# Gate and up products of an expert block in turn, one pair of weights each, in a diffusion backbone on one core

## The chip, the cores and the metric

The kernel runs on 1 core of one Trainium2 chip. The metric is the device time of one execution in microseconds (us); a median over executions is given, and the profile is of one execution. The computation is all in float32.

## The reference

A two-layer backbone over 256 latent tokens and 256 context tokens of width 1024. Layer 0 mixes by latent attention and pooling and has a dense SwiGLU of width 2816. Layer 1 mixes by a 2-D Fourier transform and has a mixture of eight experts of width 3584, of which each token uses two. A final RMSNorm follows. The case is about the experts:

```python
def swiglu(h, w1, w3, w2):
    return (jax.nn.silu(h @ w1) * (h @ w3)) @ w2

def moe_swiglu(h, router_w, w1, w3, w2):
    logits = (h @ router_w).astype(jnp.float32)
    top_v, top_i = lax.top_k(logits, TOP_K)
    top_p = jax.nn.softmax(top_v, axis=-1)
    gates = jnp.sum(jax.nn.one_hot(top_i, N_EXPERTS, dtype=jnp.float32) * top_p[..., None],
                    axis=-2).astype(h.dtype)
    y = jnp.zeros_like(h)
    for e in range(N_EXPERTS):
        y = y + gates[..., e:e + 1] * swiglu(h, w1[e], w3[e], w2[e])
    return y
```

`w1` gives the gate product, `w3` the up product, `w2` the down product. The weights of one expert are 44 MB, of all eight 352 MB.

## The kernel before

The first 400 us or so compute layer 0, the Fourier mixing of layer 1, the router, and gather the tokens of the first four experts. Then the expert stage begins, and it runs to the end but for some 15 us of final norm and output.

**Places.** The experts are computed in eight places, one after the other, in two groups of four (`expert`, called from line 2412 for the first group and line 2419 for the second). An expert's tokens are gathered into 96 slots, three groups of 32 (`QUAD`). Places 1, 3 and 7 are light: they take 64 slots, two groups of 32. The others are called heavy here. A second round of places, for experts with more tokens, isn't run on these inputs.

**Blocks and pairs.** An expert's width of 3584 is cut into 7 blocks of 512. Of each block, gate, up and down weights are 2 MB each: one pair, of two halves of 1 MB. So an expert has 21 pairs, q = 0 to 20. `PAIR_AT` (line 118) says which are whose. The work of a place is in phases: up(0), the last down of the place before (`down` 3), up(1) with the combine of the place before inside it, down(0), up(2), down(1), up(3), down(2). Phases 0 to 2 have two blocks and phase 3 one. In an up phase the gate pair of a block comes first (q) and the up pair next (q + 1).

**The ring.** Pairs land in a ring of 8 slots (`SLOTS`) in on-chip memory. SP (SyncE) issues all loads in the order of use, each for the slot of the pair eight before it. The pairs of place 0 that have to wait for a slot are loaded by halves (`load_half`, line 637); from place 1 on (and for the last pair of place 0) a load is a whole pair (`load`, line 632). The loads of the first eight pairs are issued before the stage begins. SP waits on the semaphore `e_used`, which TensorE raises: 42 halves (`PIECES`) a place. `used_with` gives the count after which half s of a pair is free.

**Gate and up.** `up` (line 2335) takes both pairs of a block at once: `landed_two` is a view of two slots. The tokens are the stationary operand, 128 rows by 32 columns, and the weights are the moving one, 256 columns: 128 of the gate pair and 128 of the up pair. For each half s of the pairs, four contraction chunks k, the groups g of 32 tokens and four column groups c of the array (each taking other weight columns), there is one matmul (line 2352): 192 a block in a heavy place, 128 in a light one. Gate and up results of up to two blocks stand side by side in one PSUM bank a group, `bank[g]`. Ahead of half s TensorE waits for both pairs (`pair_wait` twice), and after it `e_used` rises by 2. So both pairs of a block come free together, and SP needs no wait of its own for the second of them (`QUAD_SECOND`).

**Down.** `down` multiplies the hidden values with one pair at a time, 512 columns a matmul (line 2367), into banks 3 and 4, and raises `e_used` by 1 a half.

**Between them.** When the last block of an up phase is done (`up_done`), ScalarE takes silu of the gate side (line 1048), VectorE multiplies with the up side (line 1708) and transposes (line 1712). The first matmul of a bank in the next up phase waits for the multiplication (`e_hidden`). A place's output is taken from the banks, multiplied with the gate values and spread back to the tokens (line 2331). Line 2321 gathers tokens. Line 1777 is a product of layer 0 with 128 moving columns. Line 1039 loads a place's gate table, from ScalarE's queue.

Of the kernel before, what the change touches and what calls it, by code (L numbers as in the profile page):

```python
# [15 lines left out]
P = 128  # L16
D = 1024
KD = D // P
# [101 lines left out]
QUAD_FIRST = tuple(at for (phase, *_), at in PAIR_AT.items() if phase == "up")  # L120
QUAD_SECOND = tuple(at + 1 for at in QUAD_FIRST)

# [93 lines left out]
def build(nc, vec_d, con_d, rope_d, x_d, ctx_d, ada_d, mixa_d, mixb_d, attn_d, mixout_d, ffn_d,  # L216
          dft_d, fnet_d, router_d, moe_d, out_d):
    ctx = ExitStack()
    with ctx:
# [29 lines left out]
        def view(t, at, *dims):  # L249

            n = int(np.prod(dims))
            v = t[:, at:at + n]
            if len(dims) == 2:
                return v.rearrange("p (a b) -> p a b", a=dims[0])
            if len(dims) == 3:
                return v.rearrange("p (a b c) -> p a b c", a=dims[0], b=dims[1])
            return v
# [194 lines left out]
        def queue_at(i, q):  # L452

            return PAIRS * i + q - 1 if i or q >= AHEAD else q
# [26 lines left out]
        def used_with(q, s, last):  # L481

            if q in QUAD_FIRST:
                return 2 * last + (2 if s == 0 else 4)
            return 2 * last + (s + 1 if q not in QUAD_SECOND else 2 * s)
# [41 lines left out]

        def landed_two(slot):

            pairs = view(ring, 0, SLOTS, 2 * PIECE)  # L530
            one, other = SLOT_AT[slot], SLOT_AT[(slot + 1) % SLOTS]
            return pairs[:, one:other + 1, :] if other > one else pairs[:, one::other - one, :]
# [57 lines left out]
        def _(sp):  # L590
# [93 lines left out]
            def expert_loads(e, before, i, group, j):  # L684

                for q in range(PAIRS):
                    if q == 0 and j == 0 and not isinstance(group, int):
                        sp.wait_ge(e_used, PIECES * i - 2)
                    elif (q + PAIRS - SLOTS) % PAIRS not in QUAD_SECOND:
                        sp.wait_ge(e_used, PIECES * i + used_with((q + PAIRS - SLOTS) % PAIRS, 1, q - SLOTS - 1))  # L690
                    load(slot_of_pair(group, j, q), before if q == AHEAD else e, q)
# [3 lines left out]
            for (phase, *_), q in PAIR_AT.items():  # L695
                for s, n in ([(s, queue_at(0, q) + d) for s in range(2) for d in range(2)] if phase == "up" else
                             [(s, queue_at(0, q) + d) for d in range(1 if q == AHEAD else 2) for s in range(2)]):
                    if SLOTS <= n < BY_HALVES and q != AHEAD:
                        left = n - SLOTS
                        sp.wait_ge(e_used, used_with(left if left < AHEAD else left + 1, s, left))  # L700
                        load_half(n, s)
# [11 lines left out]
            freed = sp.value_load(loops[0:1, 2:3], min_val=PIECES * EXPERTS - 2 * SLOTS + 2, max_val=PIECES * EXPERTS * MAX_ROUNDS)  # L713
# [370 lines left out]
        def _(dve):  # L1084
# [435 lines left out]
            def cols(at, n):  # L1520
                return small[:, at:at + n]
# [89 lines left out]
            def gates():  # L1611
# [27 lines left out]
                link(nc.vector.tensor_scalar(cols(213, 1), cols(210, 1), float(PIECES * EXPERTS), float(PIECES * EXPERTS - 2 * SLOTS + 2),  # L1639
# [118 lines left out]
        def _(pe):  # L1758
# [576 lines left out]
            def up(i, j, phase, block, first, light, group):  # L2335

                blocks = 1 if phase == 3 else 2
                q = PAIR_AT["up", phase, block]
                weights = landed_two(slot_of_pair(group, j, q)).rearrange("p z (s k h a c r) -> p z s k h a c r", s=2, k=4, h=2, a=2, c=2)
                for s in range(2):  # L2340
                    if j == 0 and phase == 0 and block == 0:
                        pe.wait_ge(x_first, KD // 2 * group + 2 * s + 2)
                        pe.wait_ge(x_second, KD // 2 * group + 2 * s + 2)
                    for side in range(2):
                        pair_wait(pe, group, j, q + side, s)
                    for k in range(4):
                        for g in range(slots_of(light)):
                            if block == 0 and s == 0 and k == 0 and not (first and phase == 0):
                                pe.wait_ge(e_hidden, PHASES * TRIPLES * i + TRIPLES * (phase - 1) + g + 1)
                            for c in range(4):  # L2350
                                out = bank[g][c * QUAD:(c + 1) * QUAD, 0:2 * blocks * P].rearrange("p (z b n) -> p z b n", z=2, b=blocks)
                                last = mm(out[:, :, block, :].rearrange("p z (a r) -> p z a r", a=2),  # L2352
                                          x_group[:, 4 * s + k, j * CAP + g * QUAD:j * CAP + (g + 1) * QUAD],
                                          weights[:, :, s, k, c // 2, :, c % 2, :],
                                          start=(block == 0 and s == 0 and k == 0), stop=(s == 1 and k == 3 and block == blocks - 1), skip_group_check=True)
                    last.then_inc(e_used, 2)
# [140 lines left out]
```

## Time and profile before

| What | us |
|---|---|
| Median of 3 runs | 1247.53 |
| Lowest and highest | 1246.42, 1248.97 |
| The profiled execution | 1248.82 |
| Span of its profile | 1247.0 |

The page of a profile gives each engine's busy time, then the span in 40 equal slices (31.2 us each) with the rate of the transfers, the DMA queues, the chain of work that ended last, and groups of instructions by line. "PE" is TensorE's matmuls, "PEld" its weight loads, "SPq" SP's queue of DMA issues. In a group, "x9408" is a count, then come busy time and the mean length of one; matmuls overlap, so busy time divided by the count is the pace of them, and the mean length is more. "Idle before" is idle time of the engine ahead of the group, with what ended it. In the chain, "issue" is time in which the engine waited for nothing that the profile shows. A wait for two semaphores is put down to one of them.

Of the DMA queues, q1 holds what SP issues (weights), q10 what ScalarE issues (gate tables), q8 the instructions of the program. "DMA to landing" is the time from SP's issue of a load until all of it is in.

### The profile page before, as it was taken

The page shows a single profiled execution, that of the slowest core. Times are in us where ns is not written, and L with a number is a line of the kernel's source. Part 1 is how long each engine was busy: PE and PEld are TensorE (multiplying, and loading weights), DVE is VectorE, ACT ScalarE, POOL GpSimd, SP SyncE. Part 2 cuts the span into 40 slices and gives each one's busy share as a digit, 9 for nine tenths or more (in the row PEclk, how much of TensorE's full clock was granted, in tenths as well). Part 3 has the DMA queues.
Part 4 walks back from the last instruction along what each step waited for, and adds up shares of the span by engine and source line. Part 5 has one row for each costly group of instructions (what it writes and reads, how often), then busy time and mean ns, then how long its engine had stood idle before and what let it go on. Part 6 is the DMA issues. An engine that isn't in the chain of part 4 may idle for free.

```text
span 1247.0 us, 33411 instructions
## 1 busy us (share of the span) xinstructions
PE 1189.7 (95%) x15405; PEld 766.4 (61%) x15405; DVE 429.7 (34%) x853; ACT 222.9 (18%) x375; POOL 16.6 (1%) x34
## 2 busy tenths in 40 slices
PE   8999999999999999998999997799999999999977
PEld 6767999999997654453555554455555545555533
DVE  3588699999866101010020020112002011200203
ACT  4375543334433000000000000000000000000002
POOL 0400000000000000000000000000000000000000
PEclk8999999999999999998999999899999999999989
DMA  9963799988845899999999999999999999999992
GB/s 385 350 240 110 274 390 357 356 342 333 329 172 203 353 377 382 422 420 427 426 425 426 426 424 428 427 423 427 426 425 422 399 418 405 414 403 425 425 426 119
DMA packets 39548, 460.08 MB, mean 369 GB/s; under 512 B 4592, under 2 KB 4976, under 8 KB 7024
## 3 DMA queue, kind: packets, MB, share of 16 engines
q1 hardware_dynamic: 38064, 455.77, 88.9%
q8 instruction: 122, 2.00, 0.6%
q10 hardware_dynamic: 1344, 2.16, 0.5%
q14 instruction: 18, 0.15, 0.0%
HBM read 456.81 MB, written 1.11 MB: 367 GB/s over the span
## 4 chain that ended last, share of the span: by engine, by line
PE 70%; DVE 14%; DMA 11%; issue 3%; ACT 1%; DVEq 0%; SPq 0%; ACTq 0%
PE bank L2352 37%; PE bank L2367 18%; DMA ring<-in_moe 9%; DVE work L1161 6%; DVE split L1145 4%; PE bank L1885 4%; PE bank L1957 1%; PE bank L1777 1%; PE bank L2331 1%; PE bank L2321 1%; DMA ring<-in_ada 1%; DMA ring<-in_fnet 1%; DVE ring L1435 1%; DVE split L1446 1%; PE bank L2093 1%
## 5 line engine op out<-in xcount | busy, mean ns | idle before, releaser
L2352 PE MATMUL bank<-ring,work 128*32 128x256 f32 x9408 | 525.9, 384 | 36.6 <-issue 22.1
L2352 PEld LDWEIGHTS bank<-ring,work 128*32 128x32 f32 x9408 | 313.5, 111 | 254.0 <-issue 65.3
L2367 PE MATMUL bank<-ring,moe 128*32 128x512 f32 x2352 | 258.2, 592 | 0.0
L1708 DVE TENSOR_TENSOR moe<-moe,bank 128x256 f32<-128x256 f32 (+1 forms) x84 | 28.2, 384 | 621.8 <-ACT moe L1048 621.8
L2367 PEld LDWEIGHTS bank<-ring,moe 128*32 128x32 f32 x2352 | 77.6, 110 | 161.6 <-issue 154.5
L1048 ACT ACTIVATE moe<-bank 128x256 f32<-128x256 f32 (+1 forms) x84 | 24.4, 357 | 746.2 <-PE bank L2352 746.2
L2178 PE MATMUL bank<-split 128*128 128x256 f32 x1024 | 125.4, 283 | 0.8 <-DVE split L1145 0.7
L2178 PEld LDWEIGHTS bank<-split 128*128 128x128 f32 x1024 | 123.8, 192 | 1.6 <-DVE split L1145 1.2
L1145 DVE TENSOR_TENSOR split<-ring,split 128x2048 fp32r<-128x2048 f32 x33 | 75.5, 2289 | 7.4 <-ACT split L941 3.3
L1161 DVE SCALAR_TENSOR_TENSOR work<-ring,condp,work 128x512 f32<-128x512 f32 x98 | 73.6, 752 | 4.1
L941 ACT ACTIVATE split<-ring 128x2048 fp32r<-128x2048 f32 x31 | 59.3, 1914 | 74.8 <-PE bank L2178 72.6
L2168 PE MATMUL bank<-split 128*128 128x256 f32 x480 | 59.4, 283 | 0.0
L2168 PEld LDWEIGHTS bank<-split 128*128 128x128 f32 x480 | 58.3, 192 | 0.4 <-issue 0.4
L1885 PE MATMUL bank<-split 128*128 128x256 f32 x384 | 47.5, 284 | 0.0
L1885 PEld LDWEIGHTS bank<-split 128*128 128x128 f32 x384 | 46.4, 192 | 1.4 <-issue 1.4
L1694 DVE SCALAR_TENSOR_TENSOR xT<-bank,ada,xT 128x256 f32<-128x256 f32 x64 | 25.9, 476 | 53.5 <-PE bank L2331 53.5
L1100 DVE TENSOR_TENSOR split<-ring,split 128x1024 fp32r<-128x1024 f32 (+1 forms) x24 | 27.8, 1175 | 7.5 <-ACT split L786 7.2
L786 ACT ACTIVATE split<-ring 128x1024 fp32r<-128x1024 f32 (+1 forms) x24 | 24.0, 1017 | 32.4 <-PE bank L1885 18.2
L1712 DVE STREAM_TRANSPOSE moe<-moe 128x256 f32<-128x256 f32 (+1 forms) x84 | 28.2, 382 | 0.0
L1957 PE MATMUL bank<-split 128*128 128x256 f32 x168 | 25.8, 305 | 1.1 <-ACT split L815 0.9
L1957 PEld LDWEIGHTS bank<-split 128*128 128x128 f32 x168 | 21.6, 189 | 4.0 <-issue 3.5
L1686 DVE SCALAR_TENSOR_TENSOR split<-bank,small,split 128x512 fp32r<-128x512 f32 x16 | 11.3, 747 | 30.5 <-ACT split L1023 30.5
(279 smaller groups left out, 619.3 us busy)
## 6 DMA issues: line engine op xcount, KB each, us to landing
ring<-in_moe SPq DMA_DIRECT2D x148, 2048.0 KB, 23.6
ring<-in_moe SPq DMA_DIRECT2D x40, 1024.0 KB, 8.9
ring<-in_ffn SPq DMA_DIRECT2D x16, 2048.0 KB, 8.1
ring<-in_ada SPq DMA_DIRECT2D x28, 1024.0 KB, 7.1
ring<-in_ada SPq DMA_DIRECT2D x10, 2048.0 KB, 10.1
ring<-in_mixout SPq DMA_DIRECT2D x2, 2048.0 KB, 8.2
ring<-in_fnet SPq DMA_DIRECT2D x2, 2048.0 KB, 10.0
ring<-in_mixa SPq DMA_DIRECT2D x2, 1024.0 KB, 15.9
```

The source lines that it names most:

```text
L941: nc.scalar.activation(high_d[:, q % SPLITS_DENSE, :], piece_view(q), ACT.Copy).then_inc(high_ready, 1)
L1100: nc.vector.tensor_tensor(mixer_part(m, 1), mixer_source(m), plain(mixer_part(m, 0)), ALU.subtract).then_inc(mixer_low, 1)
L1145: nc.vector.tensor_tensor(low_d[:, q % SPLITS_DENSE, :], piece_view(q), plain(high_d[:, q % SPLITS_DENSE, :]), ALU.subtract).then_inc(low_ ...
L1161: ins = nc.vector.scalar_tensor_tensor(out=total, in0=half_view(h)[:, k, :], scalar=weight, in1=total, op0=ALU.mult, op1=ALU.add)
L1708: nc.vector.tensor_tensor(gate_e[:, g, 0:n], gate_e[:, g, 0:n], bank[g][:, n:2 * n], ALU.mult).then_inc(e_hidden, counts_for(light, g))
L1712: nc.vector.transpose(hiddenT[phase % 2][:, g, 0:n].rearrange("p (a s r) -> p a s r", s=2, r=QUAD), gate_e[:, g, 0:n].rearrange("p (a r s) ...
L1885: last = mm(bank[banks[c // 2]][:, (c % 2) * T:(c % 2) * T + T], parts[left][:, k, j * P:(j + 1) * P], source[right][:, k0 + k, :], start= ...
L1957: last = mm(out, parts[left][:, k, lo:hi], h_in[right][:, k0 + k, 0:n], start=((left, right) == PRODUCTS[0] and k0 + k == 0 and opens), st ...
L2168: last = mm(bank[FFN_BANKS[k // 2]][:, (k % 2) * T:(k % 2) * T + T], w[:, j, k * P:(k + 1) * P], hidden_parts[g % 2][:, right, j, :], star ...
L2178: last = mm(bank[kind == "w3"][:, j * T:(j + 1) * T], w[:, k, j * P:(j + 1) * P], h_parts[:, right, k, :], start=(n == 0 and j == 0 and k ...
L2352: last = mm(out[:, :, block, :].rearrange("p z (a r) -> p z a r", a=2), x_group[:, 4 * s + k, j * CAP + g * QUAD:j * CAP + (g + 1) * QUAD] ...
L2367: last = mm(bank[3 + n][c * QUAD:(c + 1) * QUAD, :], hiddenT[phase % 2][:, g, blk * QUAD:(blk + 1) * QUAD], weights[:, s, j, n * 512:(n + ...
```

## The change

The gate product of a block is computed in full from its pair, and then the up product from the other: the loop over `side` is outside the loops over halves and chunks. A matmul has 128 columns in place of 256, and there are twice as many. Each half waits for its own pair alone and raises `e_used` by 1. The columns at which results stand in PSUM stay the same. `QUAD_FIRST`, `QUAD_SECOND` and `landed_two` go, `used_with` becomes a plain count, SP waits before every load, and the halves of place 0 are loaded in plain order. The constant for the very last load follows the new count.

```diff
-        def used_with(q, s, last):
-
-            if q in QUAD_FIRST:
-                return 2 * last + (2 if s == 0 else 4)
-            return 2 * last + (s + 1 if q not in QUAD_SECOND else 2 * s)
+        def used_with(last, s):
+
+            return 2 * last + s + 1
...
                 for q in range(PAIRS):
                     if q == 0 and j == 0 and not isinstance(group, int):
                         sp.wait_ge(e_used, PIECES * i - 2)
-                    elif (q + PAIRS - SLOTS) % PAIRS not in QUAD_SECOND:
-                        sp.wait_ge(e_used, PIECES * i + used_with((q + PAIRS - SLOTS) % PAIRS, 1, q - SLOTS - 1))
+                    else:
+                        sp.wait_ge(e_used, PIECES * i + used_with(q - SLOTS - 1, 1))
                     load(slot_of_pair(group, j, q), before if q == AHEAD else e, q)
...
-            for (phase, *_), q in PAIR_AT.items():
-                for s, n in ([(s, queue_at(0, q) + d) for s in range(2) for d in range(2)] if phase == "up" else
-                             [(s, queue_at(0, q) + d) for d in range(1 if q == AHEAD else 2) for s in range(2)]):
-                    if SLOTS <= n < BY_HALVES and q != AHEAD:
-                        left = n - SLOTS
-                        sp.wait_ge(e_used, used_with(left if left < AHEAD else left + 1, s, left))
-                        load_half(n, s)
+            for n in range(SLOTS, BY_HALVES):
+                for s in range(2):
+                    sp.wait_ge(e_used, used_with(n - SLOTS, s))
+                    load_half(n, s)
...
             def up(i, j, phase, block, first, light, group):
 
                 blocks = 1 if phase == 3 else 2
-                q = PAIR_AT["up", phase, block]
-                weights = landed_two(slot_of_pair(group, j, q)).rearrange("p z (s k h a c r) -> p z s k h a c r", s=2, k=4, h=2, a=2, c=2)
-                for s in range(2):
-                    if j == 0 and phase == 0 and block == 0:
-                        pe.wait_ge(x_first, KD // 2 * group + 2 * s + 2)
-                        pe.wait_ge(x_second, KD // 2 * group + 2 * s + 2)
-                    for side in range(2):
-                        pair_wait(pe, group, j, q + side, s)
-                    for k in range(4):
-                        for g in range(slots_of(light)):
-                            if block == 0 and s == 0 and k == 0 and not (first and phase == 0):
-                                pe.wait_ge(e_hidden, PHASES * TRIPLES * i + TRIPLES * (phase - 1) + g + 1)
-                            for c in range(4):
-                                out = bank[g][c * QUAD:(c + 1) * QUAD, 0:2 * blocks * P].rearrange("p (z b n) -> p z b n", z=2, b=blocks)
-                                last = mm(out[:, :, block, :].rearrange("p z (a r) -> p z a r", a=2),
-                                          x_group[:, 4 * s + k, j * CAP + g * QUAD:j * CAP + (g + 1) * QUAD],
-                                          weights[:, :, s, k, c // 2, :, c % 2, :],
-                                          start=(block == 0 and s == 0 and k == 0), stop=(s == 1 and k == 3 and block == blocks - 1), skip_group_check=True)
-                    last.then_inc(e_used, 2)
+                for side in range(2):
+                    q = PAIR_AT["up", phase, block] + side
+                    weights = landed(slot_of_pair(group, j, q)).rearrange("p (s k h a c r) -> p s k h a c r", s=2, k=4, h=2, a=2, c=2)
+                    for s in range(2):
+                        if j == 0 and phase == 0 and block == 0 and side == 0:
+                            pe.wait_ge(x_first, KD // 2 * group + 2 * s + 2)
+                            pe.wait_ge(x_second, KD // 2 * group + 2 * s + 2)
+                        pair_wait(pe, group, j, q, s)
+                        for k in range(4):
+                            for g in range(slots_of(light)):
+                                if block == 0 and side == 0 and s == 0 and k == 0 and not (first and phase == 0):
+                                    pe.wait_ge(e_hidden, PHASES * TRIPLES * i + TRIPLES * (phase - 1) + g + 1)
+                                for c in range(4):
+                                    at = (side * blocks + block) * P
+                                    last = mm(bank[g][c * QUAD:(c + 1) * QUAD, at:at + P].rearrange("p (a r) -> p a r", a=2),
+                                              x_group[:, 4 * s + k, j * CAP + g * QUAD:j * CAP + (g + 1) * QUAD],
+                                              weights[:, s, k, c // 2, :, c % 2, :],
+                                              start=(block == 0 and side == 0 and s == 0 and k == 0),
+                                              stop=(s == 1 and k == 3 and block == blocks - 1), skip_group_check=True)
+                        last.then_inc(e_used, 1)
```

## Rows read from the trace of the kernel before

**Rows 1.** The page, its head and TensorE's busy time
```profile
span 1247.0 us, 33411 instructions
...
PE 1189.7 (95%) x15405; PEld 766.4 (61%) x15405; DVE 429.7 (34%) x853; ACT 222.9 (18%) x375; POOL 16.6 (1%) x34
```

**Rows 2.** The page, GB/s moved in each of the 40 slices
```profile
GB/s 385 350 240 110 274 390 357 356 342 333 329 172 203 353 377 382 422 420 427 426 425 426 426 424 428 427 423 427 426 425 422 399 418 405 414 403 425 425 426 119
```

**Rows 3.** Engines by windows, place 0, with clock, DMA share and GB/s
```profile
core 0: us, PE busy (x) PEld busy (x) DVE busy (x) ACT busy (x) POOL busy (x), PEclk, DMA share, GB/s
400.00:410.00 10.00, 10.00 (x183) 5.97 (x185) 5.40 (x29) 3.13 (x4) 0.00 (x0) 1.00 0.31 104
410.00:420.00 10.00, 10.00 (x192) 6.00 (x187) 0.00 (x0) 0.00 (x0) 0.00 (x0) 1.00 0.81 306
...
440.00:450.00 10.00, 10.00 (x133) 4.10 (x128) 2.09 (x6) 0.94 (x3) 0.00 (x0) 1.00 0.81 278
```

**Rows 4.** The chain that ended last: start, length, what
```profile
484.99 10.36 PE bank L2352 x192
...
571.46 4.98 issue
...
1181.67 29.42 DMA ring<-in_moe
...
1211.32 9.90 PE bank L2352 x128
1221.21 10.35 PE bank L2367 x96
```

**Rows 5.** TensorE's groups by line from 808 to 1109 us
```profile
L2352 PE MATMUL bank<-ring,work 128*32 128x256 f32 x3840 | 209.9, 379 | 0.0
```

**Rows 6.** Groups of the whole span; the third is one burst on the timeline
```profile
L2352 PE MATMUL bank<-ring,work 128*32 128x256 f32 x9408 | 525.9, 384 | 36.6 <-issue 22.1 <-DMA ring<-in_moe 13.5 <-DVE moe L1708 1.1
...
L1777 PE MATMUL bank<-ring,condp 128*32 128x128 f32 x512 | 17.0, 287 | 0.2 <-DMA ring<-in_ada 0.2
...
22.49 1.96 PE L1777 MATMUL bank<-ring,condp 128*32 128x128 f32 x64
```

**Rows 7.** Line 632's loads: issued from 500.5, at 500.7, at 1197.5, and all
```profile
L632 SPq DMA_DIRECT2D ring<-in_moe x142: 332/333/1462, 500.7 to 1197.5; - x142
DMA to landing us min/median/max: 10.6/24.0/36.2
...
DMA to landing us min/median/max: 14.3/14.3/14.3
...
DMA to landing us min/median/max: 28.3/28.3/28.3
...
DMA to landing us min/median/max: 7.6/23.6/36.2
```

**Rows 8.** DMA queues from 500 to 1226 us, then q8 of the whole span
```profile
q1 hardware_dynamic: 20670, 300.92, 98.2%
q10 hardware_dynamic: 1008, 1.84, 0.7%
q8 instruction: 81, 1.33, 0.7%
...
q8 instruction: 122, 2.00, 0.6%
```

**Rows 9.** DMA queues from 600 to 900 us: packets, MB, share of 16 engines
```profile
q1 hardware_dynamic: 8672, 126.32, 99.2%
q8 instruction: 34, 0.56, 0.8%
q10 hardware_dynamic: 432, 0.79, 0.7%
```

**Rows 10.** By windows, the end of the last load (columns as in rows 3)
```profile
1221.00:1223.00 2.00, 2.00 (x24) 0.61 (x20) 1.32 (x6) 0.45 (x2) 0.00 (x0) 1.00 0.54 229
1223.00:1225.00 2.00, 2.00 (x24) 0.58 (x20) 0.53 (x2) 0.00 (x0) 0.00 (x0) 1.00 0.16 66
```

More of the change, by code:

```diff
@@ L119 @@
            ("up", 2, 0): 11, ("up", 2, 1): 13, ("down", 1): 15, ("up", 3, 0): 17, ("down", 2): 19}
-QUAD_FIRST = tuple(at for (phase, *_), at in PAIR_AT.items() if phase == "up")
-QUAD_SECOND = tuple(at + 1 for at in QUAD_FIRST)
 Y_ROWS = ((1, 1, 2, 0), (0, 1, 2, 2))
@@ L526, in landed @@
             return view(ring, SLOT_AT[slot] * 2 * PIECE, 2 * PIECE)
[L528 to L532, printed above, removed]
         def by_rows(t, f):
@@ L712, in _ @@
                             expert_loads(seated(GROUP * side + j), before, GROUP * group + j, group, j)
-            freed = sp.value_load(loops[0:1, 2:3], min_val=PIECES * EXPERTS - 2 * SLOTS + 2, max_val=PIECES * EXPERTS * MAX_ROUNDS)
+            freed = sp.value_load(loops[0:1, 2:3], min_val=PIECES * EXPERTS - 2 * SLOTS, max_val=PIECES * EXPERTS * MAX_ROUNDS)
             last = seated(EXPERTS - 1)
@@ L1638, in gates @@
                 link(nc.vector.tensor_scalar(cols(212, 1), cols(210, 1), 1.0, None, ALU.add))
-                link(nc.vector.tensor_scalar(cols(213, 1), cols(210, 1), float(PIECES * EXPERTS), float(PIECES * EXPERTS - 2 * SLOTS + 2),
+                link(nc.vector.tensor_scalar(cols(213, 1), cols(210, 1), float(PIECES * EXPERTS), float(PIECES * EXPERTS - 2 * SLOTS),
                                              ALU.mult, ALU.add))
```

## The prediction, made before the changed kernel was run

> **What bounds the kernel now.** I read the page first: TensorE is busy 95% of 1247.0 us, which looks like its limit [rows 1], but from about 500 us to the end the transfers run at one flat level, 422 to 428 GB/s in most slices [rows 2]. That stretch is the expert stage, which must bring in the expert weights in pairs of 2 MB through a ring of 8 slots. So two things can bound it: the transfers, or TensorE, which gives the slots back. The table by windows shows which at its start: 104, 306 and 278 GB/s in three stretches of 10 us in which TensorE is fully busy [rows 3]. There the DMA engines wait for slots. The chain of waits then shows the rest. In place 0 (96 tokens' columns) one block of gate and up takes 10.36 us for 192 matmuls, 54.0 ns each. In the light places TensorE waits for transfers: a load is in at 571.46, and from there comes "issue" of 4.98 us, about the time of one more pair: the block waits for both of its pairs, and the second lands 4.9 us after the first [rows 4]. From 808 to 1109 us (places 4, 5 and most of 6) TensorE never waits [rows 5]; at the end it waits again, for a load issued at 1181.67, until 1211.09 [rows 4].
>
> How full are the transfers? From 500 to 1226 us the DMA engines spend 98.2% on weights, 0.7% on gate tables, 0.7% on instructions [rows 8]. And the landings give the pace: the load issued at 500.7 took 14.3 us (landed 515.0), the last, issued at 1197.5, took 28.3 (1225.8), and there are 142 of them: 710.8 / 141 = 5.04 us per pair [rows 7]. So the end is set by the pace of landings, also through the heavy places, and TensorE has 1225.8 to 1231.6 left to do after it [rows 4].
>
> **The change, part by part.** Gate and up of a block are multiplied one after the other, each from its own pair, 128 columns a matmul; a slot is handed back when its own pair has been read, and a pair is waited for alone.
>
> *Matmul time.* 9408 gate/up matmuls of 256 columns [rows 6] become 18,816 of 128, with as many weight loads. The same form (128x32 stationary, 128 columns) is in the trace: 64 in 1.96 us [rows 6]. Taking off the 0.29 us of the last one's own length and dividing by the 15 steps between groups of four gives 0.111 us a step, 28 ns each, against 27.0 ns for half of a 54.0 ns matmul. Low bound: no difference. High bound: 1.96 / 64 = 30.6 ns. I take 28: a block in a heavy place takes 0.4 us more, 2.7 us for the seven of a place. It stays under the transfers' pace where these bind. Its only part on the path is place 0, where it delays the last hand-backs by 0 to 2.7 us; I take 1, nearer the low end, since a burst of 16 steps includes its own start. The Trainium skill (TensorE: Matmul & The Clock Gate, Back-to-back issue gap) says that in a stream of loads and matmuls the spacing is set by both, 81 ns at 128 columns where the isolated gap would be 56. That speaks against this change; by that ratio the 27.0 ns would be 39, an estimate. The trace does not agree for this form, in which four column groups are used side by side: 28 ns against 27.0.
>
> *Slots handed back earlier (gain).* Now both pairs of a block come free together; after, the first comes free half a block (5.2 us) sooner, and in the first 12 loads of place 0, cut in halves of 1 MB, each half after 2.6 us. TensorE frees a pair each 5.2 us in place 0, slower than the transfers need, so after the change the queue stays almost empty there and a load lands as fast as any: 7.6 us is the least in the trace. Before, the load issued at 500.7, at the end of place 0, took 14.3 [rows 7]. That is a lead of 6.7 us when the light place 1 starts and the transfers begin to bind. Off it go the 1 us above and 1.5 us for an instruction fetch that may be in front of a load on its engine: 4.2 us. High bound 6.7; low bound 2.7, if only the half block (5.2) is won and both come off it. Later in the stage hand-backs are not what binds: before 1109 the loads queue for 20 us and more, median 24.0 [rows 7]. SP now waits before each load, where the second of a block's pairs needed no wait; behind it on SP stand only later weight loads, each needing a later release, so nothing is held up. ACT's and VectorE's waits are for the end of a block's last pair, as before: nothing.
>
> *Instructions (loss).* 9408 more matmuls and 9408 more weight loads make 18,816 more instructions beside 33,411 [rows 1]. These 33,411 came in 122 packets of 16 KB on the same DMA engines [rows 8], 274 each. After place 0 there are 8064 of the 9408 matmuls (each heavy place has 1344), so 16,128 more instructions, 59 more packets, in a stretch whose engines are 99.6% taken by the three queues [rows 8]. Price of a packet: the 81 packets there took 0.7% of 16 engines in 726 us, 1.0 us each. Evenly spread that is 1.0 / 16 = 0.063 us of the pace per packet, 3.7 us: the low bound. But a pair has landed only when all 16 engines have done their part. In the 300 us from 600, 126.32 MB took 99.2 of 100.7 parts of the time, so a pair alone costs 300 x 0.985 / 60.2 = 4.91 us [rows 9]; the landings came every 5.04. The excess is 0.13 x 141 = 18.6 us; tables are 0.7% of 726 = 5.1; 13.5 us are left for 81 packets, 0.17 us each. A few engines carry the fetches and are late: at the end of the last load the rate falls in steps, 229 GB/s, then 66, before it stops [rows 10]. I take 0.17: 59 x 0.17 = 10.0 us later. High bound 0.2 (11.8 us), if the tables spread evenly.
>
> *The wait split in two.* In the starved places TensorE starts a block 4.9 us sooner, on its first pair, and then waits in the middle of it: the stall moves to the second pair and nothing comes earlier, since the next pair is not there. Place 4's start does come sooner, but the landings bound the end. Only the last block counts. Now it starts at 1211.32, at a clock that has fallen (9.90 us for 128 matmuls), and 96 matmuls of 10.35 us follow [rows 4]; TensorE is done 5.8 us after the last landing. After, half of the block is done before its second pair lands, and what must follow the last landing is one pair of the down product, a third of 10.35 = 3.5 us. Gain 2.3 us; low bound a loss of 1.1 (that pair at half clock, 6.9 us), if the new waits in between let the clock fall.
>
> **Sum.** 10.0 - 4.2 - 2.3 = +3.5 us on the profiled execution's 1248.82 us (1247.0 of span, 1.8 around it). The median of the three runs, 1247.53, lies 1.3 below that, so I forecast 1251.0 for the median. By the spacing that the Trainium skill gives, TensorE would set the end, as in the third rival below. With all bounds: 3.7 - 6.7 - 2.3 = -5.3 to 11.8 - 2.7 + 1.1 = +10.2.
>
> **The rivals.** (1) *Faster: the earlier slots win.* If the added packets spread over all 16 engines, or fall on those that are early, they cost 3.7 us, and the lead (6.7) and the tail (2.3) outweigh them: -5.3, 1242.2 us. It decides below 0.11 us a packet. For it: only the even 1.0 us of a packet; against it: the excess in the landings and the stepped end. (2) *No change:* near 0.11 us a packet the terms cancel, 6.5 - 4.2 - 2.3 = 0, 1247.5 us. (3) *Weight loads set TensorE's pace:* with half the columns to a load, the load of the next group can set the step; at 30.6 ns the 4032 matmuls of the three heavy places 4 to 6 take 7.2 ns more each, +29 us on a TensorE that has no idle there [rows 5], less about 3 of its earlier start: some 1273. It decides from about 28 ns on, where 2.0 ns x 4032 less 3 is 5 us, as much as the landings lose. By the spacing of the Trainium skill (same page and section) it would be 12 ns a matmul of 128 columns, 97 us, an estimate. Against: the row gives 28 once its ends are taken off, but it is a burst of 64, not a stream of 768. (4) *TensorE runs out of instructions:* 274 now last 137 matmuls of 54 ns (7.4 us), after 3.7 us. If a fetch turns round in more than 3.7 us, each of 59 or more packets costs up to another 3.7, so up to 218 us. Nothing in the trace shows the turn-round, only that 7.4 us is enough.
>
> **How the numbers follow.** Forecast (slower by about 3.5) 0.48; rival 1 0.22; rival 2 0.20; rival 3 0.06; rival 4 0.04. 0.2% is 2.5 us, about what a measurement can tell from no change. Faster 0.22, same 0.20, slower 0.58. The range goes from rival 1's time, 1 us inside it, to the forecast's upper bound, 1247.5 + 10.2 = 1258, and 4 us into the start of rivals 3 and 4: 1243 to 1262.
>
> **What the profile will show.** Right: gate/up matmuls x18816 of 128x128 with a block near 10.6 us; no slice under 380 GB/s between 410 and 500 us; loads issued near 500 us landing in 8 to 10 us; some 195 instruction packets; landings every 5.1 us after 515; TensorE ending 3.5 us after the last landing. Wrong: the same number of packets or a landing pace still at 5.04 (rival 1), TensorE's block over 11.5 us (rival 3), TensorE idle on "issue" inside blocks with its slots landed (rival 4).

## The result and the profile after

The changed kernel takes 1446.17 us (median of 4 runs), against 1247.23 us for the kernel before beside it: 1.159 of the time, interval [1.157, 1.161]. It is 199 us slower, where 3.5 were forecast. Its profiled execution has a span of 1440.1 us.

The page after, its head, the 40 slices (36.0 us each) and the instruction queue:

```profile
span 1440.1 us, 52188 instructions
PE 1252.9 (87%) x24813; PEld 1040.2 (72%) x24813; DVE 430.5 (30%) x853; ACT 222.9 (15%) x375; POOL 17.3 (1%) x34
...
GB/s 361 338 176 176 391 349 363 337 314 198 300 260 340 286 335 383 400 426 366 267 295 362 405 426 400 317 254 291 350 326 270 303 367 255 285 326 371 403 401 39
...
q8 instruction: 195, 3.19, 0.8%
...
PE 72%; issue 13%; DVE 12%; ACT 1%; DMA 1%; DVEq 0%; SPq 0%; ACTq 0%
...
ring<-in_moe SPq DMA_DIRECT2D x148, 2048.0 KB, 9.6
```

Against [rows 1, 2, 8]: 18,777 more instructions in 73 more packets, near what was counted beforehand (18,816 more instructions; 59 packets after place 0, where 64 came: 145 from 525 us on, against 81). But the flat 425 GB/s of the expert stage is gone (254 to 426), and a load lands in a median of 9.6 us where it queued for 24.0 [rows 7]. So the transfers have stopped being the bound. The chain that ended last has 1% of DMA left and 13% of "issue", time in which TensorE waits for nothing that the profile shows.

TensorE's groups from 400 to 1426 us, where the expert stage lies (x count, busy us, mean ns, then idle before and its releaser):

```profile
L2339 PE MATMUL bank<-ring,work 128*32 128x128 f32 x18816 | 579.0, 281 | 155.8 <-issue 154.2 <-DVE moe L1695 1.0
L2355 PE MATMUL bank<-ring,moe 128*32 128x512 f32 x2352 | 279.2, 612 | 10.1 <-issue 10.1
```

Gate and up take 579.0 + 155.8 = 734.8 us where they took 525.9 + 36.6 = 562.5 [rows 6]: 172 us more, of which 119 us are idle time, nearly all of it on "issue", and 53 us busy time. The down product, whose instructions are unchanged, took 258.2 us busy with no idle before; now it takes 289.3, 31 us more. Together that is 203 us, about the whole of the loss (193 of span). In these groups no wait ends with the landing of a load any more. A part of the busy time is the clock: the one granted was 0.96 in the mean from 500 to 1100 us, and behind a row of stops it falls. The 128 matmuls from 680.24 us took 5.20 us, with a mean of 0.72 granted from 680 to 686 us, so a part of it at the lower level of 1.2 GHz; most stretches of 128 take 3.70.

Where in the code does TensorE stop? Its timeline in place 2 of the changed kernel:

```profile
644.25 3.70 PE L2339 MATMUL bank<-ring,work 128*32 128x128 f32 x128 [2.79 <-issue]
650.46 3.70 PE L2339 MATMUL bank<-ring,work 128*32 128x128 f32 x128 [2.51 <-issue]
656.67 3.70 PE L2339 MATMUL bank<-ring,work 128*32 128x128 f32 x128 [2.51 <-issue]
662.06 3.37 PE L2339 MATMUL bank<-ring,work 128*32 128x128 f32 x115 [1.69 <-issue]
665.16 0.59 PE L2355 MATMUL bank<-ring,moe 128*32 128x512 f32 x1
665.23 0.31 PE L2339 MATMUL bank<-ring,work 128*32 128x128 f32 x3
665.33 1.71 PE L2355 MATMUL bank<-ring,moe 128*32 128x512 f32 x9
667.72 2.35 PE L2355 MATMUL bank<-ring,moe 128*32 128x512 f32 x19 [0.68 <-issue]
```

A word on counts first: the loops of `up` make 96 float32 matmuls a block in a heavy place, and the trace records 192, two for each; all counts of matmuls here are the trace's, and so are the instructions. TensorE runs 128 matmuls and stops, time after time, at places that have nothing to do with a half (96 matmuls of 128 columns), a pair (192) or a block (384). With their 128 weight loads these are 256 instructions, and a packet of 16 KB has room for 256 if one is 64 bytes; the page's counts give 52188 / 195 = 268 for all engines. The starts are 6.21 us apart, and 3.70 us of that are work. The count runs on across the lines: 115 + 1 + 3 + 9 = 128 matmuls of both products, then the next stop, inside the down product. The queue of instructions (q8) keeps the same time: its packets stand at 641.8, 648.0, 654.2 and 659.6 us, each within 0.2 us, which is 2.3 to 2.5 us ahead of the four starts, and the second and third come just when the stretch before has ended (647.95 and 654.16). So my reading: the program arrives in packets, one at a time, and TensorE uses one up in 3.5 us. Here a period is the work on one packet and then the fetch of the next. The reading was tested as theory 1, against theory 2, that the single waits and hand-backs of the pairs cost the time.

### The profile page after: what moved, and what is told of

The parts are those of the page before. It is cut to its first block, busy times and chain, and to the rows that moved or that the text cites. A ratio compares the mean times of both kernels' runs of the same rounds, so it can differ in the third digit from the quotient of the medians.

```text
span 1440.1 us, 52188 instructions
## 1 busy us (share of the span) xinstructions
PE 1252.9 (87%) x24813; PEld 1040.2 (72%) x24813; DVE 430.5 (30%) x853; ACT 222.9 (15%) x375; POOL 17.3 (1%) x34
## 4 chain that ended last, share of the span: by engine, by line
PE 72%; issue 13%; DVE 12%; ACT 1%; DMA 1%; DVEq 0%; SPq 0%; ACTq 0%
PE bank L2339 39%; PE bank L2355 18%; DVE work L1148 5%; DVE split L1132 4%; PE bank L1872 3%; PE bank L1944 2%; PE bank L2318 1%; PE bank L1764 1%; PE bank L2308 1%; DMA ring<-in_fnet 1%; DVE ring L1422 0%; DVE split L1433 0%; PE bank L2080 0%; DVE work L1146 0%; PE bank L2066 0%
## 5 line engine op out<-in xcount | busy, mean ns | idle before, releaser
L2339 PE MATMUL bank<-ring,work 128*32 128x128 f32 x18816 | 579.0, 281 | 155.8 <-issue 154.2
L2339 PEld LDWEIGHTS bank<-ring,work 128*32 128x32 f32 x18816 | 543.6, 113 | 197.5 <-issue 191.0
L2355 PE MATMUL bank<-ring,moe 128*32 128x512 f32 x2352 | 279.2, 612 | 10.1 <-issue 10.1
L2355 PEld LDWEIGHTS bank<-ring,moe 128*32 128x32 f32 x2352 | 125.4, 113 | 137.9 <-issue 100.4
L2165 PE MATMUL bank<-split 128*128 128x256 f32 x1024 | 125.4, 283 | 0.9 <-DVE split L1132 0.9
L2155 PE MATMUL bank<-split 128*128 128x256 f32 x480 | 59.4, 283 | 0.0
L1872 PE MATMUL bank<-split 128*128 128x256 f32 x384 | 47.5, 284 | 0.0
L1087 DVE TENSOR_TENSOR split<-ring,split 128x1024 fp32r<-128x1024 f32 (+1 forms) x24 | 27.8, 1176 | 7.5 <-ACT split L773 7.2
L773 ACT ACTIVATE split<-ring 128x1024 fp32r<-128x1024 f32 (+1 forms) x24 | 24.0, 1017 | 28.9 <-PE bank L1872 18.2
L1944 PE MATMUL bank<-split 128*128 128x256 f32 x168 | 25.8, 305 | 1.1 <-ACT split L802 0.9
L2318 PE MATMUL bank<-split 128*128 128x256 f32 x128 | 19.3, 306 | 3.4 <-issue 1.8
```

Of the source, the lines that this page charges most:

```text
L1872: last = mm(bank[banks[c // 2]][:, (c % 2) * T:(c % 2) * T + T], parts[left][:, k, j * P:(j + 1) * P], source[right][:, k0 + k, :], start= ...
L1944: last = mm(out, parts[left][:, k, lo:hi], h_in[right][:, k0 + k, 0:n], start=((left, right) == PRODUCTS[0] and k0 + k == 0 and opens), st ...
L2155: last = mm(bank[FFN_BANKS[k // 2]][:, (k % 2) * T:(k % 2) * T + T], w[:, j, k * P:(k + 1) * P], hidden_parts[g % 2][:, right, j, :], star ...
L2165: last = mm(bank[kind == "w3"][:, j * T:(j + 1) * T], w[:, k, j * P:(j + 1) * P], h_parts[:, right, k, :], start=(n == 0 and j == 0 and k ...
L2318: last = mm(bank[PART_BANKS[pair]][:, (k % 2) * T:(k % 2) * T + T], y_parts[n][:, k * P:(k + 1) * P], spread[:, k // 4, :], start=(n == 0) ...
L2339: last = mm(bank[g][c * QUAD:(c + 1) * QUAD, at:at + P].rearrange("p (a r) -> p a r", a=2), x_group[:, 4 * s + k, j * CAP + g * QUAD:j * C ...
```

## The experiments

### The kernel before with twice the instructions

```diff
-                            for c in range(4):
+                            for z, c in ([(z, c) for z in range(2) for c in range(4)] if True else [(None, c) for c in range(4)]):
...
-                                          weights[:, :, s, k, c // 2, :, c % 2, :],
...
+                                    moving = weights[:, z, s, k, c // 2, :, c % 2, :]
```

> The kernel before, with its pairs, waits and hand-backs as they were; only each gate/up matmul of 256 columns is two of 128, one after the other for the four column groups: 18816 matmuls and 18816 weight loads. Theory 1, TensorE runs out of instructions (a packet of 256 instructions lasts 3.5 us of products and a new one comes each 5.4 to 6.2 us): as slow as the changed kernel, 1425 to 1460 us, with idle on 'issue' after each 128 matmuls. Theory 2, the single pair waits and hand-backs cost the time: as the kernel before, 1245 to 1255 us.

Measured: 1449.93 us (one run, as all that are given here without an interval), the slow-down in full, beside 1246.06 for the kernel before. Its groups:

```profile
L2359 PE MATMUL bank<-ring,work 128*32 128x128 f32 x18816 | 585.0, 284 | 174.5 <-issue 173.0 <-DVE moe L1708 1.0
L2372 PE MATMUL bank<-ring,moe 128*32 128x512 f32 x2352 | 266.2, 596 | 5.7 <-issue 5.7
```

Waits and hand-backs are those of before, and the idle time on "issue" is there. The order of gate and up, and the single pairs, are not needed for it.

### The changed kernel with as few instructions as before

```diff
-                        for k in range(4):
+                        for k in (0, 2):
...
-                                              weights[:, s, k, c // 2, :, c % 2, :],
+                                              weights[:, s, k:k + 2, c // 2, :, c % 2, :],
```

> The changed kernel with its single pair waits and hand-backs, but each gate/up matmul reads 256 columns of two contraction chunks of one pair, with the tokens of the first of the two, so that there are 9408 again, of the time of before. It leaves out the products of the odd chunks with their own tokens and puts them in other columns. Theory 1: no slow-down; the earlier hand-backs and the split wait show alone, 1239 to 1247 us. Theory 2: 1400 us or more.

Measured: 1241.28 us, 0.9962 of the kernel before, interval [0.9948, 0.9976]. Theory 2 is dead: with all the single waits and hand-backs of the change, and 9408 matmuls, the kernel is 4.8 us faster than before. Its windows in place 0 and its loads issued between 495 and 506 us:

```profile
400.00:410.00 10.00, 10.00 (x192) 6.04 (x188) 4.05 (x22) 1.49 (x2) 0.00 (x0) 1.00 0.78 288
410.00:420.00 10.00, 9.32 (x176) 5.33 (x164) 0.19 (x1) 0.61 (x3) 0.00 (x0) 1.00 0.99 390
...
440.00:450.00 10.00, 10.00 (x112) 3.51 (x108) 2.09 (x6) 0.94 (x3) 0.00 (x0) 1.00 0.99 358
```

```profile
L622 SPq DMA_DIRECT2D ring<-in_moe x2: 332/332/333, 498.7 to 503.9; - x2
DMA to landing us min/median/max: 9.8/9.9/10.0
```

The three stretches that moved 104, 306 and 278 GB/s [rows 3] now move 288, 390 and 358, and a load at the end of place 0 lands in 9.9 us in place of 14.3 [rows 7]: a lead of 4.4 us, where 4.2 was forecast. The landing itself, of the 142nd load from the last in both kernels, comes 6.4 us sooner (about 508.6 against 515.0), but 2.0 us of that are a stage that began sooner in this execution (398.40 against 400.37). The forecast tail of 2.3 us did not come. The end of its chain:

```profile
1187.49 31.43 DMA ring<-in_moe
1218.92 0.12 issue
1219.04 1.92 PE bank L2355 x16
1220.96 2.02 issue
1222.98 1.96 PE bank L2355 x16
```

TensorE is done 6.0 us after the last landing (5.8 before): a stop of 2.0 us on "issue" in the middle of the last pair takes the place of what was gained. It does not go with a half of the pair: in the last two kernels below, with another layout, it comes after 11 of the 32 matmuls, not 16. In all three an instruction packet stands in its queue 2.4 to 2.8 us ahead of the next matmul (at 1220.4 us here). So it looks like one more fetch, but no run tested that.

### How much fetching can TensorE bear

The kernel before, with only a part of its gate/up matmuls split in two. 1 in 8, then 1 in 4:

```diff
+                            for z, c in ([(z, c) for z in range(2) for c in range(4)] if (s == 1 and k == 3) else [(None, c) for c in range(4)]):
```

> The kernel before, with the last contraction chunk of the second half split into two matmuls of 128 columns: 1 in 8 of the gate/up matmuls, so 1176 more matmuls and loads. A packet of 256 instructions then lasts 6.1 us in the up products in place of 6.9, about the pace at which packets came in the changed kernel. Theory 1 (packets come each 5.4 to 6.2 us): the threshold is just reached, 1247 to 1262 us. Theory 2 or a price per packet on the transfers alone: 1246 to 1249 us.

Measured: 1248.61 us, 1.0014 of before, interval [1.0003, 1.0024]. Both theories allowed that.

> As the one with 1 in 8, but 1 in 4 (chunk 3 of both halves): 2352 more matmuls and loads; a packet lasts 5.5 us in the up products. Theory 1: past the threshold, the cost rises more than in proportion, 1260 to 1300 us. If the cost were in proportion to the instructions (a quarter of 200 us): 1297 us for this one and 1272 for 1 in 8.

Measured (the condition is `k == 3`): 1251.91 us, 1.0040, interval [1.0026, 1.0055]. That is less than I expected. Its groups hardly wait more than before:

```profile
L2359 PE MATMUL bank<-ring,work 128*32 128x256 f32 (+1 forms) x11760 | 532.8, 340 | 37.7 <-issue 22.9 <-DMA ring<-in_moe 13.7 <-DVE moe L1708 1.1
```

1 in 8 costs about 2 us, 1 in 4 about 5, all of them about 200: 25% more gate/up instructions cost 0.4%, 100% more cost 16%. A packet lasts 6.9 us in a block of the kernel before, 5.5 with 1 in 4, 3.5 with all. My expectation compared these with the pace at which packets came, and forgot the down product, whose matmuls take 107 ns each. Over two blocks and the down product behind them, 1 in 4 wants a packet each 6.9 us (576 matmuls in 31.1 us), more than the 5.4 to 6.2 at which they came; the changed kernel would want one each 4.7 us (864 matmuls in 31.6 us), an estimate with TensorE always fed. That fits the measured costs: what counts is the pace over such a stretch, with a store to bridge a block. Below the pace at which packets come the cost is small. The prediction's 0.17 us a packet would give 1.5 us for 1 in 8 (9 more packets, 131), where 1.9 was measured, and 3.2 us for 1 in 4 (19 more, 141), where 5.2 was. What these few us are was not separated.

### What makes a fetch slow

The changed kernel with whole-pair loads of 64 rows, then 16 rows, then half the columns:

```diff
-                sp.dma_start(landed(slot).rearrange("p (s c) -> p s c", s=2), pair_of(e, q)).then_inc(piece_in[slot][0], 16)
+                sp.dma_start(landed(slot)[0:64, :].rearrange("p (s c) -> p s c", s=2), pair_of(e, q)[0:64]).then_inc(piece_in[slot][0], 16)
```

> The changed kernel, but whole-pair loads of expert weights bring 64 of the 128 rows, 1 MB in place of 2 (the other rows keep what was there). Theory 1a, a fetch of instructions has a turn-round of its own: packets still each 5.2 to 5.6 us in the up products, 1380 to 1430 us. Theory 1b, a fetch is slow because it stands behind weight packets on its engine: packets each 4 us or less, 1290 to 1340 us. Theory 2: with loads landing early nothing is waited for, about 1230 us.

Measured: 1480.77 us, slower still and above every case that I had expected. The experiment missed its aim: half the bytes, but not half the load. The engines' share stays high (0.77) at half the rate. Windows of the changed kernel, then of this one (columns as in rows 3; before the rate stands the DMA share):

```profile
500.00:1100.00 600.00, 493.94 (x12280) 391.09 (x12272) 62.92 (x178) 21.90 (x60) 0.00 (x0) 0.96 0.89 347
```

```profile
500.00:1100.00 600.00, 485.16 (x11640) 389.02 (x11632) 58.21 (x164) 21.89 (x60) 0.00 (x0) 0.92 0.77 168
```

and the fetches themselves take longer: 90 packets are 1.2% of 16 engines there, 1.3 us each, where 96 are 1.0% and 1.0 us in the changed kernel. Why 64 rows move so slowly stays open.

> As the one with 64 rows, but 16 rows a load, 0.25 MB: nearly no weight traffic. Theory 1a: packets still each 5.2 us or more, 1370 us or more. Theory 1b: the gaps inside the up products go, TensorE runs at its own pace, 1190 to 1240 us.

Measured: 1270.93 us. Window and group:

```profile
500.00:1100.00 600.00, 571.88 (x15201) 464.66 (x15197) 76.25 (x218) 26.58 (x74) 0.00 (x0) 1.00 0.29 57
```

```profile
L2339 PE MATMUL bank<-ring,work 128*32 128x128 f32 x18816 | 543.5, 274 | 42.8 <-issue 41.2 <-DVE moe L1695 1.0
```

That lies between the two cases, 1190 to 1240 and 1370 or more. With the DMA engines busy for 0.29 of the time the idle of 155.8 us shrinks to 42.8. The edit leaves the loads by halves in place 0 as they were: 13.5 of the 42.8 us lie before 525 us. From there on 136.9 us have become 29.3. The same program, the same packets; so most of a fetch's turn-round comes with the traffic of the weights.

> The changed kernel, but whole-pair loads bring half the columns of all 128 rows, 1 MB in packets half as long, so that the DMA engines are truly about half busy. Theory 1b (a fetch waits behind weight packets): between the changed kernel and the one with 16 rows, 1290 to 1380 us, packets each 4.6 to 5.4 us.

The loads bring `[:, :, 0:PIECE // 2]` of all 128 rows; the other columns stay what they were. Measured: 1345.8 us, in the range. Window and group:

```profile
500.00:1100.00 600.00, 532.37 (x13614) 426.79 (x13606) 68.47 (x196) 24.38 (x69) 0.00 (x0) 0.98 0.63 195
```

```profile
L2339 PE MATMUL bank<-ring,work 128*32 128x128 f32 x18816 | 559.6, 277 | 98.2 <-issue 96.7 <-DVE moe L1695 1.0
```

DMA share 0.29, 0.63 and 0.89; idle before gate/up 42.8, 98.2 and 155.8 us (29.3, 85.2 and 136.9 from 525 us on). It rises with the load of the DMA engines, but at 0.29 it is not nothing. Theory 1b holds for most, and a remainder of its own stands. The share alone does not decide: the kernel with 64 rows has 171.0 us of this idle time (156.0 from 525 us on) at a share of 0.77, with its packets of 1.3 us.

The kernel before with 16 rows (the same edit) says how much the remainder is:

> The kernel before with whole-pair loads of 16 rows, nearly no weight traffic: what TensorE takes with 256 columns when neither transfers nor instructions hold it up. Theory 1: 1190 to 1205 us, so that the changed kernel with 16 rows (1270.9) still pays 65 to 80 us for its instructions, at a turn-round of its own. If the 128-column products were slower for another reason than instructions, the block would be slow in its unbroken stretches too, which are at 28 ns a matmul.

Measured: 1199.10 us. Its groups:

```profile
L2352 PE MATMUL bank<-ring,work 128*32 128x256 f32 x9408 | 515.2, 379 | 1.1 <-DVE moe L1708 1.1
L2367 PE MATMUL bank<-ring,moe 128*32 128x512 f32 x2352 | 258.0, 592 | 0.0
```

So with little traffic after place 0 the 128-column form still costs 72 us (1270.9 - 1199.1): 42 of idle and 28 of busy time in the gate/up groups, and 7 in the down product. That is 77 in all; the 5 us between are not accounted for. The 28 us are 28.9 ns a matmul (543.5 / 18816, short breaks in it) against 27.4 for half of the wide one. A stretch without a break, 128 in 3.70 us, is (3.70 - 0.27) / 31 = 0.111 us per four, as the burst of layer 0 had foretold. These two kernels had a granted clock of 1.00. So of the 53 us of busy time that the change adds to gate and up, 28 are the form, and the other 25, an estimate, the clock that falls behind the stops: 579.0 - 543.5 = 35.5 us above the kernel with 16 rows, where the kernel before has 525.9 - 515.2 = 10.7.

### Gate and up in turn in a few blocks

`up` of the changed kernel for the last block of phases 1 to 3 in place 0 and for the last block of place 7, the old one elsewhere, with SP's waits to match:

```diff
+IN_TURN = (7, 13, 17)
+LAST_IN_TURN = True
...
+                if first and q in IN_TURN or LAST_IN_TURN and phase == 3 and j == GROUP - 1 and not isinstance(group, int):
+                    return up_in_turn(i, j, phase, block, first, light, group)
```

> The kernel before, with gate and up in turn only in three blocks of place 0 (the last of phases 1, 2 and 3) and in the last block of place 7: 704 more matmuls, their slots handed back one by one. Theory 1: few enough not to run TensorE out of instructions for long (about 1.5 us a block), and the early hand-backs give the transfers most of the lead seen with 256 columns: 1241 to 1246 us. If even a single block in turn costs its starvation: 1248 to 1254 us.

Measured: 1260.00 us, 1.0105, interval [1.0088, 1.0122]. Both my cases were too low. Its chain through place 0:

```profile
432.96 6.81 PE bank L2358 x240
439.77 2.49 issue
442.26 5.13 PE bank L2358 x128
447.39 0.24 issue
...
468.94 5.67 PE bank L2358 x206
474.61 1.77 issue
476.38 3.70 PE bank L2358 x128
480.08 2.77 issue
...
496.39 6.45 PE bank L2358 x236
502.83 1.22 issue
504.05 3.70 PE bank L2358 x128
507.75 2.77 issue
```

A store of 206 to 240 matmuls' instructions is there when a block starts; after it come stops of 1.2 to 2.8 us and one of 0.24. A single block of 384 is too long for the store: two stops each, 2.7 to 4.5 us, and place 0 is where TensorE is the bound. The stretch of 5.13 us ran at a mean granted clock of 0.73 (442 to 448 us). The 704 added matmuls cost 13 us, of which these six stops are 11.3; 2352 spread over all blocks (1 in 4) cost 5. That standing in a row makes the difference is read from the stops, not tested by itself.

### The gain without the instructions

If pairs are handed back singly because each holds one half of the contraction of both gate and up, a matmul of 256 columns reads one pair. Only the host's layout and the view change, and the counts of `e_used` with them:

```diff
-            order += [(w, block, half) for block in blocks for w in ("w1", "w3") for half in range(2)]
+            order += [(w, block, half) for block in blocks for half in range(2) for w in ("w1", "w3")]
...
-                    weights = landed(slot_of_pair(group, j, q)).rearrange("p (s k h a c r) -> p s k h a c r", s=2, k=4, h=2, a=2, c=2)
+                    weights = landed(slot_of_pair(group, j, q)).rearrange("p (z k h a c r) -> p z k h a c r", z=2, k=4, h=2, a=2, c=2)
```

> The whole computation with 9408 gate/up matmuls of 256 columns and pairs handed back singly: the weights are laid out by the host so that a block's first pair holds the first half of the contraction of both gate and up, the second pair the other half. Each matmul then reads gate and up columns of one pair. Theory 1: no starvation (as many instructions as before) and the early hand-backs are kept, as in the kernel with 256 columns of one pair: 1239 to 1244 us, about 5 us under the kernel before. Theory 2: as slow as the changed kernel.

Measured: 1242.40 us, 0.9966, interval [0.9952, 0.9979]. The rows of a weight half are interleaved over the partitions, so this order pairs weights with tokens' rows other than the reference does; bytes, instructions and waits are the intended ones. The next layout takes the interleaving into account:

```diff
+            order += [("up", block, (s, a)) for block in blocks for s in range(2) for a in range(2)]
...
+        of["up"] = {(b, (s, a)): np.stack([of[w][b, a][s::2] for w in ("w1", "w3")], axis=1).reshape(P, PIECE)
+                    for b in range(BLOCKS) for s in range(2) for a in range(2)}
```

> The whole computation, with 9408 gate/up matmuls of 256 columns and pairs handed back singly. The weights are laid out so that a block's first pair holds, for gate and up alike, the rows that the matmuls of the first half s read, the second pair those of the other half. Theory 1: as the kernels with 256 columns and single pairs, 1239 to 1244 us, about 4 to 5 us under the kernel before, with some 122 instruction packets. Theory 2: as slow as the changed kernel.

Measured: 1243.17 us (10 runs), 0.9977 of the kernel before, interval [0.9965, 0.9989]: the full computation, 3.3 us under the kernel before. Its page:

```profile
span 1240.3 us, 33383 instructions
...
q8 instruction: 122, 2.00, 0.6%
```

As many instruction packets as before, and the earlier hand-backs. It is the fastest of the kernels here that compute the whole; the gain is small, and 4 to 5 us were expected.

## Why the prediction was wrong

**The count was right, its price was not.** 59 more packets were forecast after place 0 and 64 came; 195 in all, as forecast. The step that failed is "Instructions (loss)": it charged a packet only for what it takes from the transfers (0.17 us), with TensorE always fed. The runs put in its place that a packet of 256 instructions comes each 5.4 to 6.2 us where TensorE is starved beside the flow of weights, and 128 narrow matmuls use it up in 3.5 to 3.7 us. TensorE stood idle on "issue" for 154 us before gate and up. That was rival 4, with a chance of 0.04 and a price bounded at 218 us; 199 came, a part of them from the form (28 us) and from the falling clock, which rival 4 did not have. The sign named for it, idle time on "issue" inside blocks with the slots landed, is what the profile shows. Two signs named for the forecast came too: 195 packets, and loads issued near 500 us landing in 7.6 to 8.9 us; they told nothing against rival 4.

**The trace had more to say on it than I used.** I wrote that 7.4 us a packet is enough and that nothing shows the turn-round. True, but the change doubled a rate that was the highest in the trace for more than a burst (the 128-column row is 64 matmuls, half a packet), and a block of the kernel before asks for a packet each 6.9 us, where the change asks for one each 3.5. A change that leaves the region covered by any row deserved far more than 0.04.

**Matmul time: right.** 28 ns a matmul were forecast; an unbroken stretch gives 0.111 us per four. The spacing of 81 ns at 128 columns in the Trainium skill (TensorE: Matmul & The Clock Gate, Back-to-back issue gap) is not this form's: here 27.8 ns a matmul with four column groups side by side. Rival 3 falls. Where the block took longer on the whole, it was broken by stops or ran at a lower granted clock.

**Slots handed back earlier: right.** 4.2 us were forecast, 4.4 measured, by the kernel with 256 columns and single pairs. The agreement is in part luck: the forecast takes off 1 us for narrow matmuls, which that kernel does not have, and 1.5 us for a fetch, which no run shows by itself. In the changed kernel the lead is worth nothing, since the transfers no longer bind; its loads land in 9.6 us because TensorE asks for them late.

**The split wait: wrong in size.** 2.3 us forecast at the end, none measured by the kernel with 256 columns and single pairs; a stop of 2.0 us inside the last pair took it.

**The landing pace: not reached.** The excess of 0.17 us a packet is compatible with 1 in 8 and gives 3.2 of the 5.2 us of 1 in 4, but no run isolates it. Nor does any run show that few engines carry the fetches.

**The bound.** "What bounds the kernel now" held for the kernel before, and it stopped at two candidates, transfers and TensorE. The third is TensorE's program. Over two blocks and the down product the kernel before wants a packet each 8.3 us (480 matmuls in 31.1 us), against the 5.4 to 6.2 at which they come to a starved TensorE; the change wants one each 4.7.

## What to carry to other kernels

Count instructions as a stream with a rate, not only as engine time: work out how long a packet lasts TensorE before and after an edit, over the whole repeating stretch and not only its densest part, and compare it with the shortest period at which packets arrive in the trace under the same traffic. "Issue" idle time that recurs after the same number of instructions, across blocks and tiles, is a program that arrives too slowly. To hand buffers back earlier, look first for a layout that puts what one instruction reads into one buffer; splitting the instruction buys the same release with twice the program.

## What the runs showed of the hardware that I had not expected

While TensorE was starved under weight traffic, packets came each 5.4 us (409.88 to 415.25 below) to 6.2 us (644.25 to 650.46 above), though it occupies a DMA engine for only 1.0 us. TensorE's idle time before gate/up grew with the DMA engines' share, 42.8, 98.2 and 155.8 us at 0.29, 0.63 and 0.89, but the kernel with 64 rows falls out of this order (171.0 us at 0.77). Between 206 and 308 matmuls of 128 columns run unbroken after a slower stretch before the first stop; the 308 are the first ones of the changed kernel's place 0:

```profile
400.58 8.71 PE L2339 MATMUL bank<-ring,work 128*32 128x128 f32 x308
409.88 3.70 PE L2339 MATMUL bank<-ring,work 128*32 128x128 f32 x128 [0.59 <-issue]
415.25 7.20 PE L2339 MATMUL bank<-ring,work 128*32 128x128 f32 x256 [1.67 <-issue]
```

Not every start is starved: the third row is two packets' work without a stop. Loads of 64 of 128 rows kept the DMA engines busy for 0.77 of the time at 168 GB/s, slower per byte than whole ones at 0.89 and 347.
